# Gate projection as two block products of seven multiplications, with the operand sums on GpSimd and VectorE

## What is computed

```python
mod = jax.nn.silu(c) @ ada_w[l] + ada_b[l]
shift1, scale1, gate1, shift2, scale2, gate2 = [m[:, None, :] for m in jnp.split(mod, 6, axis=-1)]
h = rms_norm(x, norm1_g[l]) * (1.0 + scale1) + shift1
p = h @ w_in[l]                     # h: 1024 tokens x 1024
q, k, v, f_logit, p_rwkv, gate_logit = jnp.split(p, IN_SPLITS, axis=-1)
g_fox, g_rwkv = jnp.split(jax.nn.sigmoid(gate_logit), N_BRANCHES, axis=-1)   # gate_logit: 1024 x 2048
token_shift(p, mu) = p + (prev - p) * mu      # on p_rwkv; prev is the row above
```

## Time and profile before

| | |
|---|---|
| median of 3 runs | 1750.45 us (1749.17 to 1752.55) |
| span of the profiled execution | 1746.0 us |
| PE busy | 1612.2 us, 92% of the span |
| DVE, ACT, POOL busy | 749.2, 464.4, 354.3 us |
| narrow rwkv chunk on PE | about 324 to 357 us |
| four gate chunks on PE | about 357 to 538 us |
| attention starts | about 543 us |

### The profile page before, as it was taken

How to read it: one execution, slowest core, us unless ns; L and a number is a source line. 1 busy time by engine, 2 the same in 40 slices (tenths; PEclk the granted TensorE clock), 3 DMA queues, 4 the chain that set the end, 5 groups by cost and what they waited for, 6 DMA issues and landing times. The chain is left out here.

```text
span 1746.0 us, 33968 instructions
## 1 busy us (share of the span) xinstructions
PE 1612.2 (92%) x14322; PEld 1177.4 (67%) x14322; DVE 749.2 (43%) x1262; ACT 464.4 (27%) x899; POOL 354.3 (20%) x703
## 2 busy tenths in 40 slices
PE   5999999899998997798989999979999999999986
PEld 5688888878787884577777878846655555454442
DVE  5655455441104775688755446682111111111114
ACT  1642111121214774454542132221000000000002
POOL 1100011110002000667752011101222222121211
PEclk9999999999998998899998999999999999999998
DMA  9357765651225641232263514387999999999977
GB/s 337 134 194 277 258 209 188 211 173 68 74 87 123 153 129 41 62 75 51 53 187 118 191 50 157 124 357 282 392 404 422 422 423 422 422 423 418 402 318 300
DMA packets 144503, 398.57 MB, mean 228 GB/s; under 512 B 49027, under 2 KB 65462, under 8 KB 126944
## 3 DMA queue, kind: packets, MB, share of 16 engines
q1 hardware_dynamic: 114096, 328.77, 51.2%
q0 software_dynamic: 15504, 41.34, 6.6%
q10 hardware_dynamic: 14752, 26.29, 4.0%
HBM read 342.79 MB, written 64.17 MB: 233 GB/s over the span
## 5 line engine op out<-in xcount | busy, mean ns | idle before, releaser
L2938 PE MATMUL psum<-w,ex_x_t 128*64 128x256 f32 x1376 | 155.5, 381 | 7.0 <-DMA w<-in_exp_w 6.1
L2938 PEld LDWEIGHTS psum<-w,ex_x_t 128*64 128x64 f32 x1376 | 96.6, 137 | 59.5 <-DMA w<-in_exp_w 9.7
L167 PE MATMUL psum<-w_even,h_hi 128*128 128x512 f32 (+1 forms) x320 | 118.9, 372 | 7.3 <-ACT stage L567 7.3
L567 ACT ACTIVATE stage<-psum 128x512 f32<-128x512 f32 (+1 forms) x72 | 41.3, 574 | 302.5 <-PE psum L169 185.4
L169 PE MATMUL psum<-w_even,h_lo 128*128 128x512 f32 (+1 forms) x320 | 118.4, 370 | 0.0
L168 PE MATMUL psum<-w_even,h_hi 128*128 128x512 f32 (+1 forms) x320 | 118.3, 370 | 0.0
L3098 DVE TENSOR_TENSOR ex_sig_m<-psum,ex_sig_m 128x256 f32<-128x256 f32 x32 | 13.6, 425 | 239.8 <-ACT ex_sig_m L3062 239.8
L3062 ACT ACTIVATE ex_sig_m<-psum 128x256 f32<-128x256 f32 x32 | 12.3, 384 | 385.0 <-PE psum L2938 385.0
L167 PE MATMUL psum<-w_odd,h_hi 128*128 128x512 f32 x256 | 100.0, 391 | 0.0
L169 PE MATMUL psum<-w_odd,h_lo 128*128 128x512 f32 x256 | 99.6, 389 | 0.0
L168 PE MATMUL psum<-w_odd,h_hi 128*128 128x512 f32 x256 | 99.6, 389 | 0.0
(11 more groups left out here) (522 smaller groups left out, 3653.5 us busy)
## 6 DMA issues: line engine op xcount, KB each, us to landing
w<-in_exp_w SPq DMA_DIRECT2D x64, 2048.0 KB, 34.1
w_mixed<-in_exp_w SPq DMA_DIRECT2D x31, 2048.0 KB
w_ring<-in_ada_w SPq DMA_DIRECT2D x12, 2048.0 KB, 10.6
w_ring<-in_w_in SPq DMA_DIRECT2D x10, 2048.0 KB, 10.4
qk<-stage_r ACTq DMA_DIRECT2D x16, 512.0 KB, 7.4
gates<-stage ACTq DMA_DIRECT2D x32, 256.0 KB, 2.0
bl_gates<-gates SPq DMA_DIRECT2D x8, 1024.0 KB, 4.9
w<-pair_rows SPq DMA_DIRECT2D x16, 512.0 KB, 10.0
```

The lines of the kernel that those rows point to most:

```text
L167: nc.tensor.matmul(out, a_hi, b_hi, start=(i == 0), stop=False)
L567: nc.scalar.activation(stage[:, b, 0:n], ps[:, 0:n], ACT.Sigmoid if kind == "gate" else ACT.Copy).then_inc(sig("proj_evac"), 1)
L2938: last = mm(ps[h * MAIN:(h + 1) * MAIN, j * FH:(j + 1) * FH], x_t[:, k, 0:MAIN], w[:, k, h * FH:(h + 1) * FH], start=(k == 0), stop=(k == ...
```

## The change

The four gate chunks become two pairs. In a pair the tokens (two halves), the inner values (two halves) and the columns (two chunks) make a 2x2 product of blocks, done with seven block multiplications in place of eight. A block multiplication, here a window w = 7p + i, has four tiles of 128 tokens x 512 columns over 512 inner values: 4 x 4 x 3 = 48 matmuls. The four loads of a pair are the blocks "11", "21", "12", "22" (1 MB each).

- Operand sums of h, once for both pairs: s1 = a21 + a22 by POOL, in twelve additions of 128x512, two in front of the read-back of each of tiles m = 24 to 29; s2 = s1 - a11 by DVE (two of 128x2048); s3 and s4 by POOL, three additions of 128x2048 each, s3 after the last p_mix, s4 after s2 is split. Each sum is then split by ACT and DVE (`high_sum`, `rest`).
- Operand sums of the weights, in each pair, by DVE (`prepare`), with the split of each of the seven weight operands.
- Products come out of PSUM through DVE, which adds them up in `u2` and `u3` (`evict`); ACT takes the sigmoid and issues the DMA (`finish_row`).
- Eight gate tiles per chunk become rows of blocks; the narrow chunk keeps its high and low weights in half of `w_even`, and `w_odd` holds s1 and s2.
- s4 and some output buffers take the place of the modulation rows: rows 0 to 3 go to memory (`mods`) and are read back, spread over the partitions, in `attend`. The biases of the rows are added after chunk 4, and the sums over partitions are made inside chunk 5 (in front of its fifth tile) and at the start of the narrow chunk.

```diff
-    POOL = 100
+    POOL = 116
+RAW_SLOT = ({"11": 2, "21": 3, "12": 0, "22": 1}, {"11": 0, "21": 3, "12": 2, "22": 1})
+SUMS_AT = {(5, 4): range(0, 4), (6, 0): range(4, 8)}
+SUMS_OUT_AT = {(5, 5): range(0, 4), (6, 1): range(4, 8)}
...
-            weights.load(sp, range(CHUNKS, len(weights.order) - 2))
-            sp.wait_ge(sig("proj_full"), V_TILES + 16 + RWKV_TILES)
-            weights.load(sp, range(len(weights.order) - 2, len(weights.order)))
+            weights.load(sp, range(CHUNKS, len(weights.order)))
+            for role in RAW_ORDER:
+                sp.wait_ge(sig("ring_used"), len(weights.order) - (1 if role[1] == "1" else 0))
+                weights.load_raw(sp, 0, role)
...
+            def sum_s1(piece):
+                step, k = piece // HK, piece % HK
+                if piece == 0:
+                    pool.wait_ge(sig("proj_full"), 8 * NARROW)
+                if step == 2:
+                    pool.wait_ge(sig("s1_part"), HK + k + 1)
+                dst, x, y = ((s1_sum, f32(a21[0]), f32(a21[1])), (s1_more, f32(a22[0]), f32(a22[1])), (s1_sum, s1_sum, s1_more))[step]
+                add(dst[:, k, :], x[:, k, :], y[:, k, :], ALU.add).then_inc(sig("s1_part"), 1)
             for m in range(RWKV_TILES + 1):
+                if RWKV_TILES - 8 <= m < RWKV_TILES - 2:
+                    sum_s1(2 * (m - RWKV_TILES + 8))
+                    sum_s1(2 * (m - RWKV_TILES + 8) + 1)
...
+            pool.wait_ge(sig("proj_full"), 8 * len(proj))
+            pool.wait_ge(sig("s1_part"), 3 * HK)
+            add(s3_sum, f32(a11[1]), f32(a21[1]), ALU.subtract).then_inc(sig("s3_part"), 1)
...
+            pool.wait_ge(sig("mods_out"), 16)
+            pool.wait_ge(sig("s2_lo"), 1)
+            add(s4_sum, f32(a12[1]), f32(s2[1]), ALU.subtract).then_inc(sig("s4_part"), 1)
...
+            def prepare(w):
+                p, i = w // PRODUCTS, w % PRODUCTS
+                (hi, lo), total = unit[w % 2], unit_sum[w % 2]
+                q = {role: weights.raw(p, role) for role in RAW_ORDER}
+                if i in (2, 3):
+                    dve.wait_ge(sig("prod"), 4 * (w - 1))
...
+                    tt(total, q["22"], q["11"] if i == 2 else q["12"], ALU.subtract).then_inc(sig("t_sum"), 1)
+                    dve.wait_ge(sig("t_sum"), 2 * p + i - 1)
+                    if i == 2:
+                        tt(q["21"], q["21"], total, ALU.subtract).then_inc(sig("t4_sum"), 1)
+                    dve.wait_ge(sig("u_hi"), w + 1)
+                    tt(lo, total, f32(hi), ALU.subtract).then_inc(sig("u_lo"), 1)
+                    return
+                src = q[("11", "21", None, None, "21", "11", "22")[i]]
+                dve.wait_ge(sig("u_hi"), w + 1)
+                tt(lo, src, f32(hi), ALU.subtract).then_inc(sig("u_lo"), 1)
+                if i == 1:
+                    weights.raw_arrived(dve, p, "12")
+                    tt(q["11"], q["12"], q["11"], ALU.subtract).then_inc(sig("t1_sum"), 1)
...
+                    if (j, i) == (NARROW, 4):
+                        prepare(0)
...
+            for w in range(WINDOWS):
+                p, i = w // PRODUCTS, w % PRODUCTS
+                if w == 0:
+                    shift(RWKV_TILES - 1)
+                if w + 1 < WINDOWS:
+                    prepare(w + 1)
+                if w == 0:
+                    dve.wait_ge(sig("s1_part"), 3 * HK)
+                    tt(s2_sum, s1_sum, f32(a11[0]), ALU.subtract).then_inc(sig("s2_part"), 1)
+                    dve.wait_ge(sig("s2_part"), 1)
+                    tt(s2_sum, s2_sum, f32(a11[1]), ALU.subtract).then_inc(sig("s2_sum"), 1)
+                if w == 1:
+                    rest(s2, s2_sum, "s2")
...
+                for r in range(4):
+                    evict(p, i, r)
+                if w == 2:
+                    rest(s3, s3_sum, "s3")
+                if w == 3:
+                    rest(s1, s1_sum, "s1")
+                if w == 4:
+                    rest(s4, s4_sum, "s4")
...
+            for w in range(WINDOWS):
+                p, i = w // PRODUCTS, w % PRODUCTS
+                pe.wait_ge(sig("u_lo"), w + 1)
+                if p == 0 and i in (2, 3, 5, 6):
+                    pe.wait_ge(sig({2: "s2_lo", 3: "s3_lo", 5: "s1_lo", 6: "s4_lo"}[i]), 1)
...
+                for r in range(4):
...
+                    matmul3(nc, bank[b], pairs).then_inc(sig("prod"), 1)
...
+            sp.dma_start(keep["mod_bc"][:, 0:4, :].rearrange("p a n -> p (a n)"),
+                         dram["mods"].partition_broadcast(P).rearrange("p a n -> p (a n)")).then_inc(sig("mods_in"), 16)
```

More of the change, by code:

```diff
@@ L224, in flip_reader, with block_of, out_count, out_sig @@
             return n - 7 if n == 7 else n - 3 if n < KT + 2 else n - 2
+        unit = [tuple(w_even[:, i, part * HK:(part + 1) * HK, :] for part in range(2)) for i in range(2)]
+        narrow = [unit[1][part].rearrange("p k n -> p (k n)").rearrange("p (k n) -> p k n", k=KT) for part in range(2)]
+        NARROW = len(proj) - 1
         def w_of(parts, j):
+            if j == NARROW:
+                return narrow[0 if parts is w_hi else 1]
             return parts[j % 2]
+        def block_of(half, kh):
+            return tuple(h[:, kh * HK:(kh + 1) * HK, half * NC5:(half + 1) * NC5] for h in (h_hi, h_lo))
+        a11, a12, a21, a22 = (block_of(half, kh) for half in range(2) for kh in range(2))
+        s1, s2 = (tuple(w_odd[:, i, part * HK:(part + 1) * HK, :] for part in range(2)) for i in range(2))
+        s3 = a21
+        s4 = tuple(keep["s4"][:, part] for part in range(2))
+        unit_sum = [sum_even[:, i, HK:KT, :] for i in range(2)]
+        s1_sum, s1_more, s2_sum = sum_odd[:, 0, HK:KT, :], sum_odd[:, 0, 0:HK, :], sum_odd[:, 1, HK:KT, :]
+        s3_sum, s4_sum = keep["sum_h"][:, 1, 0:HK, NC5:2 * NC5], keep["sum_4"][:, 1]
+        OPERAND = (a11, a12, s2, s3, a22, s1, s4)
+        WINDOWS = PAIRS_OF * PRODUCTS
+        f32 = lambda ap: ap.bitcast(F32)
+        def out_count(b, p, second):
+            before = {0: 14, 1: 13, 2: 13}.get(b, 0)
+            return before + (2 * p + second if b == 0 else p)
+        def out_sig(b):
+            return sig(f"staged_out{b}")
+        def gate_rows(p, half, col, r):
+            rows = slice((half * 4 + r) * P, (half * 4 + r + 1) * P)
+            return dram["gates"][rows, (2 * p + col) * NC5:(2 * p + col + 1) * NC5]
         V_TILES, RWKV_TILES = TT, TT * -(-SHIFT // NC5)
@@ L566, in _ @@
                             act.wait_ge(sig("shift_sum"), m + 1)
-                        nc.scalar.activation(stage[:, b, 0:n], ps[:, 0:n], ACT.Sigmoid if kind == "gate" else ACT.Copy).then_inc(sig("proj_evac"), 1)
+                        nc.scalar.activation(stage[:, b, 0:n], ps[:, 0:n], ACT.Copy).then_inc(sig("proj_evac"), 1)
                         act.wait_ge(sig("proj_evac"), fill + 1)
@@ L782, in _ @@
                 sp.wait_ge(sig(f"o_out{b}"), 16 * N // OUT)
+            sp.wait_ge(sig("mods_in"), 16)
         @block.gpsimd
```

209 lines of the change are left out of this document (185 added, 24 removed).

## The result

The changed kernel takes 1778.56 us (median of 4 runs, 1775.09 to 1779.68) against 1751.5 us (4 runs) for the kernel before on the same chip. The ratio is 1.0149, with a 95% interval from 1.0127 to 1.0171: 27 us slower. The profiled execution took 1779.68 us, with a span of 1777.9 us, against 1746.0 us before.

A forecast was written before the change was run, and what follows sets the result against it. The prediction took PE's matmuls to bound the gate phase. PE ending at 558.3 us, 20.1 later, plus 0.7 for the last tile, was summed to +20.9 on the median 1750.45: 1771.3 us; 8-in-10 range 1751 to 1784.

The forecast's parts named there:

- Parts 1 and 2: Gate phase: 672 matmuls in place of 768, 21.8 us less; sum products wholly hidden in PE's wait, 6.9 us gained.
- Part 3: Loads and biases before the shift chain: additions counted at nothing, upper bound 5.7 us; read-back of m = 24 at 345.5.
- Part 4: POOL additions and DVE operations on two SBUF tiles exclude each other in turn; PSUM evictions free; 128x2048 on POOL 5.04 us.
- Part 5: Shift chain with two short POOL additions per tile: steps of 4.9 us, end at 381.8, as late as before.
- T: End of the shift chain in the narrow chunk, forecast at 381.8 us, bounds 375.3 to 388.
- Part 6: Way to windows 2 and 3: starts at T + 33.2 and T + 55.2; 1.6 us for each long wait.
- Part 7: From window 3 on PE never late, ends at 558.3, 20.1 us later; modulation read-back nothing, 2 us at most.
- no-lock rival: POOL's long additions run beside DVE or in its gaps: PE ends at 530.5, time 1743.4; chance 0.12.
- DVE goes first: Rival: POOL gets the port only when DVE has nothing queued; window 3 at T + 42, about 1752 us; chance 0.08.

The follow-up runs named there:

- adds_unneeded: Changed kernel with s3 and s4 filled by ScalarE copies (wrong values), plus three 128x2048 POOL additions behind the chain that no product waits for; 1768.36 us.
- before_rows_by_memory: Kernel before, with the four finished modulation rows written to memory and read back to all partitions, as the changed kernel does; 1749.23 us, ratio 1.0026.
- all_sums_by_copy: Changed kernel with no addition on POOL: ScalarE copies fill s1, s3 and s4 (wrong values); 1751.34 us.
- long_sums_on_dve: Changed kernel with the six long additions for s3 and s4 made by VectorE in place of POOL; 1764.35 us, ratio 1.0086.

## Why the prediction was right, and where it was not

The forecast was 1771.3 us, slower, 20.9 us over the median of before; measured were 27 (26.3 in the means).

- **Parts 1 and 2.** 672 matmuls, a window in 10.9 us, the sum products gone from the full stretch. Right. But the products now wait for the additions of the biases, which the text had counted only against the chain: PE waited 1.7 us (304.65) for them. This was not foreseen, and stayed hidden ahead of PE's later wait for the chain.
- **Part 3.** Read-back of m = 24 expected at 345.5, measured 345.88. Right.
- **Part 4, taking turns.** Right for the long additions, now shown by adds_unneeded and not only read off two rows; that evictions from PSUM are free, too (rows of 412.62). For the short ones it was not always so: VectorE waited for two additions in a row (rows of 348.15). The length of POOL's 128x2048 was the term that was mis-sized: 5.04 us was estimated as four times 1.26, 4.60 was measured (its lower bound was 4.4), and one addition delays VectorE by 6.69 - 2.28 = 4.4. So a part of each short operation is overhead, as 4 x 1.26 against 4.60 shows. The Trainium skill, page GPSIMD Engine Reference, section Elementwise — side-by-side cycle accounting, gives 4497 ns for this very size; the trace agrees within about 0.1 us, and with it the term would have been right.
- **Part 5.** T = 381.8 expected, 381.84 measured. That it fits so closely is luck: in the four other profiles with the same chain it ended between 380.9 and 384.2. The runs show two smaller errors behind it: the short additions cost the chain 4.6 us, not 6.5, and a slow write near its end takes the difference.
- **Part 6.** Windows 2 and 3 expected at T + 33.2 and T + 55.2, measured at T + 31.0 and T + 51.0. The order of operations was right, and window 1 started at T + 2.3 as said; three additions at 4.4 in place of 5.04 make 2 us of the first, and as much again of the second. Half clock behind a long wait was priced at 1.6 us; windows 0 and 2 took 13.6 and 13.2 us in place of 10.9 (367.75 to 381.30, 412.80 to 425.98), so it was 2.7 and 2.3. From window 3 to the end it was 122.9 us, not 121.3.
- **Part 7.** PE's end was expected at 558.3, measured 555.7: 17.5 us later than before, not 20.1. Then the step that failed: "I add the difference to the median", so all that follows was taken to shift by the same amount. The mark shifted by 19.1, and 7 to 8 us more were lost behind it, by a lower granted clock for the most part. The part also put the read-back of the modulation rows at 2 us at most; before_rows_by_memory (4.2, good to some 3 us) leaves that open.

So the mechanism and its place were right; the sum was 3 us too high in the front and nearly 9 us too low behind it, and that these two partly cancel is luck. The no-lock rival falls by adds_unneeded, "DVE goes first" by the alternating ends.

## What to carry over

An addition given to an idle POOL is not free for VectorE: where both read two inputs from SBUF they take turns, and a 2.28 us operation beside an addition of 4.60 takes 6.7. Count it where VectorE bounds, or let VectorE do it in a gap in which it waits for a DMA. Prepare the operands of the next phase between the steps of a slow chain and not behind its end; here both together turned a loss of 26 us in the mean into a gain of 12. And do not count a front shortened by x as x: here 20.0 us at the mark became 11.9 in the mean, with a later stage that keeps falling to half clock, for a reason that stayed open. Judge such changes by the mean of many runs, and look at the granted clock stage by stage and in every run.

## What the hardware showed unexpectedly

The recur stage, from the first store of the blocks of u to the third read of o_rwkv, took between 236.5 us (all_sums_by_copy) and 256.7 us (long_sums_on_dve) in the profiles, with identical instructions and 30 to 33 us of waits of PE in all of them; it was 241.8 before. Each microsecond more went with some 2.8 us more at half clock (over the 14 profiles).

The second product of the experts took 116.9, 118.6 or 120.3 us depending on the build, with the same code for it in all (rows above). Its cause was not looked for.
